# Two heads' logits and scores issued column block by column block, in a sparse-attention decoder kernel

## The reference, cut to what matters

```python
logits = jnp.einsum('bqhd,bsd->bqhs', iqb, ik) * IDX_DIM ** -0.5       # 8 indexer heads of 64
score = jnp.einsum('bqhs,bqh->bqs', jax.nn.relu(logits), iwb)          # weighted sum over heads
score = jnp.where(causal[None], score, -jnp.inf)
_, sel = lax.top_k(score, 256)                                         # 256 keys of each query
s = jnp.einsum('bqhd,bqkd->bqhk', qb, k_sel) * HEAD_DIM ** -0.5        # 6 heads of 64, one shared key
pr = jax.nn.softmax(jnp.where(valid[:, :, None, :], s, -jnp.inf), axis=-1)
out = jnp.einsum('bqhk,bqkd->bqhd', pr, v_sel)
```

## Time and profile before

| | us |
|---|---|
| runs of the kernel | 4434.04, 4434.5, 4438.0 |
| median | 4434.5 |
| span of the profiled execution, first to last instruction | 4430.7 |
| PE busy in that span | 3971.5 (90%) |
| DVE busy | 2016.5 (46%) |
| ACT busy | 1003.7 (23%) |
| POOL busy | 1008.5 (23%) |

### The profile page before, as it was taken

One profiled execution on the slowest core, in us unless ns is written; L12 is line 12 of the kernel. 1 busy time (PEld: TensorE's weight loads), 2 busy tenths in 40 slices (PEclk: granted clock), 3 DMA queues, 4 the chain that ended last, 5 costly groups with the idle time before them and its releaser, 6 DMA issues.

```text
span 4430.7 us, 52428 instructions
## 1 busy us (share of the span) xinstructions
PE 3971.5 (90%) x19064; PEld 2895.6 (65%) x19064; DVE 2016.5 (46%) x3281; ACT 1003.7 (23%) x1665; POOL 1008.5 (23%) x764
## 2 busy tenths in 40 slices
PE   7889878888899999999988888878888999999997
PEld 3445445677775788888734444557876667888885
DVE  4488884434335222222236889744334242222224
ACT  2111122332312212211121211132323121221122
POOL 1032222233212122222100512213331212222221
PEclk9888875899999999999988888769998999999999
DMA  2000000000001111111110000000000101111110
GB/s 107 27 15 15 10 15 19 1 0 0 0 29 48 48 47 47 47 52 43 38 50 16 15 10 15 10 19 1 0 0 10 57 29 43 47 47 52 47 47 38
DMA packets 35109, 128.73 MB, mean 29 GB/s; under 512 B 4128, under 2 KB 4640, under 8 KB 34080
## 3 DMA queue, kind: packets, MB, share of 16 engines
q1 hardware_dynamic: 34688, 126.01, 8.2%
q10 hardware_dynamic: 288, 1.05, 0.1%
HBM read 120.76 MB, written 5.24 MB: 28 GB/s over the span
## 4 chain that ended last, share of the span: by engine, by line
PE 57%; issue 28%; POOLq 6%; DVE 3%; DVEq 2%; POOL 2%; ACT 1%; DMA 1%; ACTq 0%; SPq 0%
PE bank L904 12%; PE bank L906 12%; PE bank L905 12%; PE bank L693 3%; PE wide L560 2%; PE bank L709 1%; DVEq L1491 1%; PE bank L637 1%; PE wide L709 1%; PE bank L703 1%; PE wide L565 1%; PE wide L703 1%; PE wide L623 1%; POOLq L1317 1%; DVE AM L1483 1%
## 5 line engine op out<-in xcount | busy, mean ns | idle before, releaser
L1316 POOL TENSOR_TENSOR WL<-WR,WH 128x1024 fp32r<-128x1024 f32 x160 | 388.8, 2430 | 1495.4 <-ACT WH L1132 1494.7
L590 PE MATMUL bank<-X,WR 128*128 128x512 f32 x1152 | 568.9, 652 | 20.4 <-ACT X L965 9.4
L904 PE MATMUL bank<-XH,WH 128*128 128x512 f32 x1280 | 517.5, 404 | 19.5 <-DVE XL L1362 10.0
L906 PE MATMUL bank<-XH,WL 128*128 128x512 f32 x1280 | 501.8, 392 | 0.0
L905 PE MATMUL bank<-XL,WH 128*128 128x512 f32 x1280 | 501.5, 392 | 0.0
L590 PEld LDWEIGHTS bank<-X,WR 128*128 128x128 f32 x1152 | 237.0, 212 | 327.3 <-issue 296.4
L904 PE MATMUL bank<-HH,WH 128*128 128x512 f32 x1024 | 400.4, 391 | 0.0
L1695 DVE TENSOR_TENSOR Y<-Y,bank 128x512 f32<-128x512 f32 x256 | 176.1, 688 | 491.9 <-PE bank L906 491.9
L906 PE MATMUL bank<-HH,WL 128*128 128x512 f32 x1024 | 398.6, 389 | 0.0
L905 PE MATMUL bank<-HL,WH 128*128 128x512 f32 x1024 | 398.5, 389 | 0.0
L1682 DVE TENSOR_TENSOR RB<-RB 128x512 f32<-128x512 f32 x128 | 88.6, 692 | 561.5 <-ACT RB L1158 561.5
(11 more groups left out here) (282 smaller groups left out, 6096.3 us busy)
## 6 DMA issues: line engine op xcount, KB each, us to landing
WR<-in_w SPq DMA_DIRECT2D x128, 512.0 KB, 3.5
WR<-in_w_in SPq DMA_DIRECT2D x36, 512.0 KB, 3.2
WR<-in_w_out SPq DMA_DIRECT2D x16, 512.0 KB, 3.5
WR<-in_w_gate SPq DMA_DIRECT2D x16, 512.0 KB, 5.5
Y<-in_xT SPq DMA_DIRECT2D x2, 2048.0 KB, 12.8
out_T<-X SPq DMA_DIRECT2D x1, 4096.0 KB, 11.1
UQ<-in_w_uq SPq DMA_DIRECT2D x2, 1024.0 KB, 7.7
PE_IN<-in_pT SPq DMA_DIRECT2D x2, 1024.0 KB, 4.8
```

What stands on the lines that cost most here:

```text
L590: mm = e.matmul(BK_[hf], WR[:, i % RING, kt, :], X[:, kt, hs(hf)], start=kt == 0, stop=kt == KT - 1)
L904: e.matmul(BK_[b], WH[:, s, w, :], high[:, kt, q], start=kt == 0, stop=False)
L906: mm = e.matmul(BK_[b], WL[:, s, w, :], high[:, kt, q], start=False, stop=kt == kts - 1)
L1316: e.tensor_tensor(WL[:, s, :, :], WR[:, i % RING, :, :], WH[:, s, :, :].bitcast(F32), ALU.subtract)
```

## The change

The order by hand puts both pv of a pair ahead of both s. On PE, the item of an even head now issues both heads of lg or of s, the first 512 columns of the one and of the other, then the rest of both; it waits for both wide banks ahead of the first matmul, and the item of the odd head issues nothing. For blocks of up to 512 columns the order of the matmuls within a pair is as before. ACT and DVE do their items at the places of the list, as before. What stands between the two items of a pair in the list (a z item for some pairs of lg and s) comes behind both on PE. Because pv and s change places, `spread_in` puts some rounds on the other side of an s: rounds 9 and 10 of block 2 ahead of block 7's head 2, for instance, and block 7's rounds 17 to 20 and a z item ahead of block 6's head 4.

```diff
--- before.py
+++ after.py
@@ -96,8 +96,8 @@
 
 
 
-ATTENTION = [("s", 0), ("s", 1), ("lg", 2), ("lg", 3), ("pt", 0), ("pt", 1), ("pv", 0), ("s", 2), ("pv", 1), ("s", 3),
-             ("lg", 4), ("lg", 5), ("pt", 2), ("pt", 3), ("pv", 2), ("s", 4), ("pv", 3), ("s", 5), ("lg", 6), ("lg", 7),
+ATTENTION = [("s", 0), ("s", 1), ("lg", 2), ("lg", 3), ("pt", 0), ("pt", 1), ("pv", 0), ("pv", 1), ("s", 2), ("s", 3),
+             ("lg", 4), ("lg", 5), ("pt", 2), ("pt", 3), ("pv", 2), ("pv", 3), ("s", 4), ("s", 5), ("lg", 6), ("lg", 7),
              ("pt", 4), ("pt", 5), ("pv", 4), ("pv", 5), ("fin", 0)]
 ROUNDS = TOPK // 8
 HEAD_START = 4
@@ -602,28 +602,38 @@
                 mm.then_inc(narrow.full, 1)
 
             def logits(L, b, h):
-                n, w, lo = (b + 1) * P, h % 2, HD * (h % 2)
+                n = (b + 1) * P
                 if h == 0:
                     e.wait_ge(narrow.free, narrow.read(L, ("iq", b)))
-                e.wait_ge(wide[w].free, wide[w].before(L, ("lg", b, h)))
+                for w in range(2):
+                    e.wait_ge(wide[w].free, wide[w].before(L, ("lg", b, h + w)))
                 for c in range(0, n, HALF):
                     c1 = min(n, c + HALF)
-                    mm = e.matmul(WIDE[w][:, c:c1], IQ[lo:lo + HD, h // 2, :], IK2[lo:lo + HD, c:c1],
-                                  start=True, stop=True)
-                mm.then_inc(wide[w].full, 1)
+                    for w in range(2):
+                        lo = HD * w
+                        mm = e.matmul(WIDE[w][:, c:c1], IQ[lo:lo + HD, h // 2, :], IK2[lo:lo + HD, c:c1],
+                                      start=True, stop=True)
+                        if c1 == n:
+                            mm.then_inc(wide[w].full, 1)
+
+            def scores_of_pair(L, b, h):
+                n = (b + 1) * P
+                if h == 0:
+                    e.wait_ge(narrow.free, narrow.read(L, ("q", b)))
+                for w in range(2):
+                    e.wait_ge(wide[w].free, wide[w].before(L, ("s", b, h + w)))
+                for c in range(0, n, HALF):
+                    c1 = min(n, c + HALF)
+                    for w in range(2):
+                        lo = HD * w
+                        mm = e.matmul(WIDE[w][:, c:c1], QT[lo:lo + HD, h // 2, :], A3[lo:lo + HD, 2, c:c1],
+                                      start=True, stop=True)
+                        if c1 == n:
+                            mm.then_inc(wide[w].full, 1)
 
             def attention(L, what, b, h):
                 n, w, lo = (b + 1) * P, h % 2, HD * (h % 2)
-                if what == "s":
-                    if h == 0:
-                        e.wait_ge(narrow.free, narrow.read(L, ("q", b)))
-                    e.wait_ge(wide[w].free, wide[w].before(L, (what, b, h)))
-                    for c in range(0, n, HALF):
-                        c1 = min(n, c + HALF)
-                        mm = e.matmul(WIDE[w][:, c:c1], QT[lo:lo + HD, h // 2, :], A3[lo:lo + HD, 2, c:c1],
-                                      start=True, stop=True)
-                    mm.then_inc(wide[w].full, 1)
-                elif what == "pt":
+                if what == "pt":
                     e.wait_ge(wide[w].free, wide[w].before(L, (what, b, h)))
                     e.wait_ge(probs_ready, L * (NB * NH) + (ATT_AT[b] * NH + h + 1))
                     for kt in range(b + 1):
@@ -831,8 +841,12 @@
                         mm.then_inc(narrow.full, 1)
                         e.wait_ge(dup_landed, L * 64 + 32 * (b + 1))
                     elif kind == "lg":
-                        logits(L, b, h)
-                    elif kind in ("s", "pt", "pv"):
+                        if h % 2 == 0:
+                            logits(L, b, h)
+                    elif kind == "s":
+                        if h % 2 == 0:
+                            scores_of_pair(L, b, h)
+                    elif kind in ("pt", "pv"):
                         attention(L, kind, b, h)
                     elif kind == "rms":
                         e.wait_ge(rms_done, L + 1)
```

## The result

The changed kernel takes 4446.96 us (median of 9 runs, 4444.02 to 4452.38) against 4434.06 of the kernel before (9 runs, 4431.5 to 4438.0): 12.9 us slower, ratio 1.0028 with a 95% interval of 1.0018 to 1.0038. A second measurement gave 1.0042 (1.0028 to 1.0055). The forecast was 4456, and the range of 4434 to 4477 holds it.

The account below looks back on a forecast made before the run. DVE was taken to bound the top-k stretch, PE's savings there being idle time. Per layer 1.4 + 1.8 + 4.8 + 4.8 - 1.0 - 1.0 = +10.8, twice +21.6, giving 4456 us, range 4434 to 4477.

Parts of the forecast that it names:

- (a): Interleaved columns inside a pair on PE: worth 0, as two heads already run fully side by side.
- Rival 4: Old order overlaps only in part; interleaving saves 0.85 us on some six pairs a layer: 4424 us, 2 in 100.
- (c): Logits wait for both banks, delaying relu and DVE's SC: +1.4, +1.8, +4.8, +4.8 us a layer in blocks 4 to 7.
- rival 2: No difference: pairs mostly at full clock, or later DVE waits absorb the delay; 4434 us within 9, 15 in 100.
- The forecast's other sign: In the top-k stretch, DVE's wait for ACT's relu grows from 16 to about 25 to 30 us a layer.
- (b): PE gets 1.3 to 3.8 us back per pair formerly run singly; 0 in the DVE-bound stretch, on the path after 655.
- block 7, by z: Heads 4, 5: z starts at the pair's end, 483.0, and ends at 492.7; odd head's SC still 2.4 us late.
- Rival 3: Slower still: z runs at 9.68 instead of 7.13 us after PE idles; +12 us a layer, 4480 us, 13 in 100.
- rival 1: Faster: pair and relu fit within one 2.4 us round, DVE's first SC covered; -10 a layer, 4414 us, 14 in 100.
- (d): Scores of head h+2 behind pv of head h+1: -1.0 us a layer after 655 us, -1.0 at block 6's last pair.
- Block 6's last pair: Its score maximum, which waited 2.12 us for PE, gets four rounds ahead of it: -1.0 us a layer.
- The full-clock bound: All pairs at 1.98 instead of 3.78 us: 1.6 off each of seven costly pairs, about 0 a layer, 4434 us.

Follow-up runs that it names:

- the cover: The changed kernel with DVE alone pulling rounds forward, at least two ahead of each even head's SC in blocks with rounds: 4418.96 us, ratio 0.9974.
- the added wait: The kernel before with one line added, the logits of an even head waiting for both wide banks: 4477.79 us, ratio 1.0105.
- head by head: The changed kernel with each pair's column blocks no longer interleaved, both waits still ahead: 4453.12 us, ratio 1.0051; measured again 4447.65 us, 1.0033.
- the scores' part alone: The changed kernel with the old head-by-head logits at their own places, scores still paired: 4424.88 us, ratio 0.9983; measured again 4425.61 us, 0.9986.
- logits' part alone: The kernel before with the logits paired as in the change, scores and pv as before: 4466.39 us, ratio 1.0075.
- odd head's wait behind the even: The head-by-head form of the changed kernel, in logits waiting for the odd head's bank only behind the even head's matmuls: 4442.13 us, ratio 1.0019.

## Why the prediction was right, and where it was not

**The bound and the sign.** DVE was the bound of the top-k stretch and PE's savings in it were idle time: shown by the cover, which on DVE alone takes 12.9 and 16.1 us off the rounds of the two layers while PE waits as before, and by the added wait, which costs 46 us without any pairing.

**(a) Interleaving, 0.** Right: 4448.47 against 4447.65 us. Rival 4 is out: the pair takes 3.79 us in either order, as one head takes 3.78. The Trainium skill (TensorE: Matmul & The Clock Gate, Part 3) says that matmuls start and end in strict program order. The trace does not agree between two heads on different halves of the rows: issued head by head, they take 3.79 us together.

**(c) The wait for both banks.** Right in place, and right in size at the SCs of blocks 5, 6 and 7. Block 5 at heads 2: forecast +2.2, found 2.1. Block 6 at heads 4 and 6: forecast +2.4 twice, found 7.20 - 4.76 = 2.4 and 9.30 - 6.87 = 2.4, where 4.76 and 6.87 are the lateness of the DVE instruction just ahead. Block 7: +2.4 twice, found 2.4 twice. Block 4: forecast +1.4, found 1.9 and 0.8 at two even heads' SCs, but only 0.2 at the end of the block: two later SCs that had waited 1.2 and 1.3 us for the relu no longer wait, which absorbs nearly all of it (the mechanism of rival 2, in this one block). The forecast's other sign of it came as well: DVE's wait for the relu, forecast at 25 to 30 us, is 27.9.

**A wait that was left out.** "DVE waits for PE or ACT only 16.0 + 4.7 us" overlooked 2.5 us at the rotated q, where DVE waits for PE's q matmuls. That wait grew: 1.1 and 1.0 us more at the rotated q behind blocks 4 and 5, for which the forecast had no term. They are no fixed part of the change: in the second profile of the same kernel they are 0.0 and 0.2 us, and head by head shows both pictures as well (0.0 and 0.2, then 1.2 and 1.0).

**(b) What PE saves.** The forecast expected matmul busy time to fall by some 30 us a layer or less; it fell by 62. Logits fell from 145.1 to 101.1 us and scores from 142.4 to 77.3 over both layers. As PE's time was not the bound, this miss did not reach the sum.

**The term mis-sized most clearly: block 7, by z.** The forecast let z run at 9.68 us behind the pair as behind the lone head, so that the odd head's SC stayed 2.4 us late. Found: z 7.94, and 1.5 of the 2.4 us came back (+11.63 to +10.11). The windows show when the clock rose. Before, then after; columns are length, PE busy, granted clock, DMA:

```profile
475.42:479.42 4.00, 4.00 (x5) 0.50 0.00 0
479.42:483.42 4.00, 4.00 (x5) 0.50 0.00 0
483.42:485.42 2.00, 2.00 (x5) 0.78 0.00 0
```

```profile
488.42:492.42 4.00, 4.00 (x9) 0.50 0.00 0
492.42:494.42 2.00, 2.00 (x4) 0.66 0.00 0
494.42:496.42 2.00, 2.00 (x6) 1.00 0.00 0
```

Behind the lone head the granted clock is 0.50 (1.2 GHz) for 8 us after PE starts again and rises in the next 2; behind the pair it is 0.66 in the stretch from 4 to 6 us and 1.00 (2.4 GHz) from then on. Block 7 costs 3.2 us and not 4.8. Rival 3, z at 9.68 us wherever it follows a pair, did not come (8.43 and 8.28 in block 6, 7.94 and 7.52 in block 7). Nor did rival 1: from the pair's start to the end of relu it takes 4.9 us (488.42 to 493.33), twice the round of 2.4 that would have had to cover it.

**(d) The tail.** The forecast was -1.0 a layer; the stairs give 8.31 - 11.27 = -2.96 for layer 1 and 15.14 - 18.12 = -2.98 for layer 2. The steps were the right ones, their sizes too small. In block 7 the second maximum comes at 688.46 against 678.44, that is 1.2 us sooner against the +11.27 of the stretch (forecast 0.75), and the next 0.4 later (forecast 0.6). At the rotated q between them 0.4 more come back, with no term in the forecast. In block 2 it is 0.8 sooner twice (forecast 0.4):

```profile
746.24 0.56 DVE L1467 CUSTOM_DVE_ANT_0 PB<-wide,WK 128x384 f32<-128x384 f32 x1 [5.95 <-PE wide L629]
747.16 0.56 DVE L1467 CUSTOM_DVE_ANT_0 PB<-wide,WK 128x384 f32<-128x384 f32 x1
```

The two maxima follow each other at 0.92 us, and the two pv in a row take less than two with an s between. Block 6's last pair was as forecast: its maximum waits 0.45 us instead of the 2.12 of the earlier trace rows.

```profile
621.29 1.09 DVE L1467 CUSTOM_DVE_ANT_0 PB<-wide,WK 128x896 f32<-128x896 f32 x1 [0.45 <-PE wide L629]
```

How much the tail gives is not fixed either: the first profiles of head by head and of the scores' part alone show -7.2 and -7.3 in layer 1, the change with the cover -7.4 and -6.6; most others with both pv ahead of both s show about -3. In the tail of layer 1 the second run of 32 pv matmuls of block 7 takes 4.56 us in the head-by-head profile and 6.93 in the change's; the granted clock there is 1.00 for 4 us in the one and 0.50 throughout in the other.

**The sum.** The forecast of +21.6 us was too high: the medians show +12.9 and, measured again, +15.8. The terms a layer, and what two profiles of the change show in layer 1:

```
term                            forecast    first    second
block 4                             +1.4     +0.2      +0.2
rotated q, three times                 0     +2.1      -0.2
block 5                             +1.8     +2.6      +2.6
block 6                             +4.8     +4.5      +4.5
block 7                             +4.8     +3.2      +3.2
block 6's last score pair           -1.0     -1.2      -1.4
tail                                -1.0     -3.0      -3.4
sum                                +10.8     +8.5      +5.6
```

Block 5 is higher than forecast because its later maxima gave back 1.9 us and not 2.5. That the sum came within 2.3 us of the first profile is in part luck: blocks 4 and 7 and the tail were set 4.8 us too high, block 5 and the missing term of the rotated q 2.9 too low. In layer 2 the two profiles give +9.1 and +6.5.

Both layers together are +17.6 in the first profile, more than the 14.5 us between the two spans. The rest lies outside the part that was changed: the changed kernel's profile is 3.1 us ahead at 104 us already, where one z item had run 9.87 us in the kernel before and 7.13 in the other, and has lost that by block 3's rotated q; it then gains 2.2 us between the two layers' stretches and 0.7 behind the second. The lead at 104 us is no effect of the change: with the same matmuls ahead of it the two head-by-head profiles are 2.9 us ahead and 1.5 behind. The later differences were not looked into.

**The full-clock bound** was no case that occurred: each pair of blocks 6 and 7 that DVE waited for ran at the half clock (3.36 and 3.79 us), after 6.4 to 11.8 us of idle PE. What spares the wait here is DVE's cover, not the clock.

## What to carry to other kernels

When two producers of an in-order engine are merged into one item, their waits are merged too: the item starts with the later one, and whoever consumes the earlier half pays, unless it has other work ordered ahead of that use. So before merging, look at the consumer's order, and before trusting a saving on the engine that is busiest in total, look which engine waits for which in the very stretch. In these runs two 64-row matmul streams on the two halves of the rows overlapped whether issued head by head or block by block (3.79 us for two heads either way); being neighbours and having both banks free was all they needed.

## What the runs showed of the hardware that was not expected

After an idle stretch the clock came back sooner when PE started with two overlapping 64-row streams than with one. Block 7's z item behind the logits of heads 4 and 5, with the idle stretch ahead of them, in us:

```
what PE starts with          idle     z      profile, layer 1
pair                        11.53    7.94    the change
pair                        11.42    7.58    head by head
pair                         9.90    7.49    logits' part alone
pair                         9.90    7.13    change with the cover
lone head                   11.34    8.80    the added wait alone
lone head                    6.12    9.68    before
two lone heads in a row      7.79    9.38    odd head's wait behind the even
```

The length of the idle stretch alone does not explain it: at 11.3 to 11.5 us of it z takes 8.80 behind a lone head and 7.58 to 7.94 behind a pair. Why is open; no run was made for it alone.
